# Two more FFN columns by seven products, single down tiles beside four columns, and a third last tile begun ahead

## The reference

```
up = rmsnorm(x) @ w_up                  # 1024 -> 2 x 2816: gate half and up half
c = conv_w3(up)                         # causal, depthwise, three taps
x = x + (silu(c_gate) * c_up) @ w_down  # 2816 -> 1024
y = rmsnorm(x)
```

## Time and profile before

| what | value |
|---|---|
| median of three runs | 858.47 us (856.91 to 859.96) |
| profiled execution, its own time | 860.1 us |
| its span, first to last instruction | 858.3 us |
| busy: PE, PEld, DVE, ACT, POOL | 839.3, 789.6, 570.7, 403.1, 124.5 us |
| mean granted clock of TensorE | 0.996 |
| first product of the first pair | 538 us |
| a pair's weight load (x<-in_w_up, 512 KB), issue to landing | 4.6 us, 30 of them |
| load of x behind the last sum (x<-scratch_x), issue to landing | 9.1 us, 2 of them |

### The profile page before, as it was taken

How to read it: one execution, slowest core, us unless ns; L and a number is a source line. 1 busy time by engine, 2 the same in 40 slices (tenths; PEclk the granted TensorE clock), 3 DMA queues, 4 the chain that set the end, 5 groups by cost and what they waited for, 6 DMA issues and landing times.

```text
span 858.3 us, 17439 instructions
## 1 busy us (share of the span) xinstructions
PE 839.3 (98%) x6800; PEld 789.6 (92%) x6800; DVE 570.7 (66%) x1005; ACT 403.1 (47%) x719; POOL 124.5 (15%) x181
## 2 busy tenths in 40 slices
PE   7999999999999999999999999999999999999995
PEld 7988877789999999877699999999999999999995
DVE  6444237578584643455354799899798998998654
ACT  7302133366353631255243665655555656656352
POOL 2320000000000000000000122323222423332100
PEclk9999999999999999999999999999999999999998
DMA  9798699721233465479232343754456656655623
GB/s 312 253 361 299 206 345 324 266 76 50 74 83 118 147 246 196 139 271 368 107 114 76 90 188 99 180 157 103 112 116 130 149 119 123 138 129 105 181 88 104
DMA packets 55188, 144.63 MB, mean 169 GB/s; under 512 B 6499, under 2 KB 9063, under 8 KB 54466
## 3 DMA queue, kind: packets, MB, share of 16 engines
q1 hardware_dynamic: 48496, 128.86, 45.3%
q0 software_dynamic: 6320, 14.53, 10.0%
q10 hardware_dynamic: 290, 0.12, 0.1%
HBM read 125.35 MB, written 18.14 MB: 167 GB/s over the span
## 4 chain that ended last, share of the span: by engine, by line
PE 81%; DMA 1%; DVE 1%; ACT 1%; issue 0%; DVEq 0%; SPq 0%
PE proj L1210 44%; PE score L1292 4%; PE score L1293 4%; PE score L1294 4%; PE T L1292 3%; PE T L1293 3%; PE T L1294 3%; PE proj L1166 2%; PE proj L1227 2%; PE proj L1229 2%; PE proj L1228 2%; PE score L1461 2%; PE score L1427 1%; DMA c_pages<-in_cache_mem_v 1%; PE T L1303 1%; PE T L1446 1%
## 5 line engine op out<-in xcount | busy, mean ns | idle before, releaser
L1210 PE MATMUL proj<-a_hi,w_hi 128*128 128x272 f32 (+1 forms) x740 | 159.8, 290 | 6.3 <-DVE w_lo L1928 6.1
L1210 PE MATMUL proj<-a_lo,w_hi 128*128 128x272 f32 (+1 forms) x740 | 158.5, 289 | 0.0
L1210 PE MATMUL proj<-a_hi,w_lo 128*128 128x272 f32 (+1 forms) x740 | 158.1, 288 | 0.0
L1561 ACT ACTIVATE w_hi<-w_raw 128x1024 fp32r<-128x1024 f32 (+2 forms) x114 | 104.6, 918 | 111.8 <-PE proj L1210 87.6
L1905 DVE TENSOR_TENSOR w_lo<-w_raw,w_hi 128x1024 fp32r<-128x1024 f32 (+2 forms) x114 | 119.8, 1051 | 30.0 <-ACT w_hi L1561 29.7
L1210 PEld LDWEIGHTS proj<-a_hi,w_hi 128*128 128x128 f32 x740 | 118.6, 190 | 12.7 <-issue 6.5
L1210 PEld LDWEIGHTS proj<-a_lo,w_hi 128*128 128x128 f32 x740 | 119.0, 190 | 0.0
L1210 PEld LDWEIGHTS proj<-a_hi,w_lo 128*128 128x128 f32 x740 | 118.7, 190 | 0.0
L1142 POOL COPY f_state<-up_pad 128x18 f32<-128x18 f32 x44 | 51.9, 1180 | 136.4 <-DVE up_pad L2061 136.4
L1857 ACT ACTIVATE p_hi<-x 128x1024 fp32r<-128x1024 f32 x30 | 31.6, 1055 | 37.4 <-PE T L1294 34.2
L1227 PE MATMUL proj<-a_hi,w_hi 128*128 128x272 f32 x160 | 48.0, 300 | 0.0
(11 more groups left out here) (364 smaller groups left out, 2055.9 us busy)
## 6 DMA issues: line engine op xcount, KB each, us to landing
x<-in_w_up SPq DMA_DIRECT2D x30, 512.0 KB, 4.6
w_raw<-in_w_in SPq DMA_DIRECT2D x21, 512.0 KB, 3.8
early_pages<-in_cache_k SPq DMA_DIRECT2D x32, 256.0 KB, 6.0
pages<-in_cache_v SPq DMA_DIRECT2D x32, 256.0 KB, 5.3
c_pages<-in_cache_mem_k SPq DMA_DIRECT2D x16, 512.0 KB, 6.6
c_pages<-in_cache_mem_v SPq DMA_DIRECT2D x16, 512.0 KB, 6.1
w_raw<-in_w_down SPq DMA_DIRECT2D x32, 256.0 KB, 2.7
w_raw<-in_w_up SPq DMA_DIRECT2D x14, 512.0 KB, 3.6
```

Source lines behind the costliest of these rows:

```text
L1210: mm = pe.matmul(tile_banks(n)[:, half, 0:width], wt, act[:, at, half * HALF:half * HALF + width], start=(k == 0 and a == 0), stop=(k == w ...
L1561: act.activation(w_hi[:, n % W_HI_RING, 0:kt, :], w_raw[:, n % W_RING, 0:kt, :], ACT.Copy).then_inc(w_hi_ready, 1)
```

## The change

`PAIRED` becomes 5 to 21, so columns 8 and 21 are computed by seven products. Down tiles stand beside columns 4 to 21, and columns 7, 8, 20 and 21 get one each. For these four a new branch gives another order: products 1, 2, down tile, 6, 5, 7, 3, 4; and on DVE output 7, then split 0 of the next pair, then its sums, then act (i-1). In column 21, which prepares no pair, act (20) stands ahead of output 7. SP's loads of raw pair weights wait for the sums too, product 6 for t_lo. Three last down tiles are begun ahead, the third in the bank pair `score`, with its weights split in column 21; w_hi and w_lo of the fourth tile come behind the start of the second.

```diff
--- before.py
+++ after.py
@@ -39,7 +39,7 @@
 GROUPS, GB = 2, 4
 SELF_UNITS = SEQ // P * HEADS
 FFN_GROUPS = [range(0, 4), range(4, 8), range(8, 12), range(12, 16), range(16, 22)]
-PAIRED = [i for i in range(5, 21) if i != 8]
+PAIRED = list(range(5, 22))
 DIST = 384
 W_RING, W_HI_RING = 4, 3
 C_PAGE_RING = 8
@@ -89,11 +89,18 @@
 
 def beside_of(i):
 
-    hosts = [c for c in range(4, 21) if c != 8]
-    if i not in hosts:
-        return []
-    g, j = divmod(hosts.index(i), 4)
-    return [(f"down{g}", "add", n) for n in (2 * j, 2 * j + 1)]
+    dealt = 0
+    for c in range(4, 22):
+        count = 1 if c in (7, 8, 20, 21) else 2
+        if c == i:
+            return [(f"down{m // KT}", "add", m % KT) for m in range(dealt, dealt + count)]
+        dealt += count
+    return []
+
+
+def by_act(q):
+
+    return (1, 5, 6, 4) if len(beside_of(PAIRED[q])) == 2 else (1, 6, 5, 4)
 
 
 def make_ffn_order():
@@ -104,7 +111,7 @@
             beside = beside_of(i)
             if i in PAIRED:
                 q = PAIRED.index(i)
-                order += [("prod", q, r) for r in (1, 2)] + beside[:1] + [("prod", q, r) for r in (5, 6)]
+                order += [("prod", q, r) for r in (1, 2)] + beside[:1] + [("prod", q, r) for r in by_act(q)[1:3]]
                 order += beside[1:] + [("prod", q, r) for r in (7, 3, 4)]
             else:
                 order += [("up", "gate", i), ("up", "up", i)] + beside
@@ -160,7 +167,7 @@
 VALUES = range(TILE["mem", "value", 0], TILE["mem", "value", KT - 1] + 1)
 FFN_FIRST = TILE[FFN_ORDER[0]]
 PRODUCTS = [(q, r) for phase, q, r in FFN_ORDER if phase == "prod"]
-BY_ACT, BY_DVE = (1, 5, 6, 4), (2, 7, 3)
+BY_DVE = (2, 7, 3)
 
 
 def make_schedule():
@@ -365,6 +372,21 @@
             s += [("prod", q, 1), ("prod", q, 2)]
             if prev_paired:
                 s += pair_ends(i - 1, q)
+            if len(downs) == 1:
+                hi0, lo0 = split_next(downs[0])
+                s += [("pair_out", q, 1), ("pair_out", q, 2), ("tile", downs[0])] + hi0 + [("taps", i - 1, 0)] + lo0
+                s += [("taps", i - 1, 1), ("gate", i - 1), ("prod", q, 6), ("prod", q, 5), ("pair_out", q, 6), ("add", downs[0])]
+                s += [("pair_out", q, 5)] + [("act", i - 1)] * (not more) + [("pair_hi", q + 1, 0)] * more
+                if i == FT - 1:
+                    s.append(("x_back",))
+                s += [("prod", q, 7), ("pair_out", q, 7)] + [("pair_split", q + 1, 0), ("sums", q + 1), ("act", i - 1)] * more + [("prod", q, 3)]
+                s += [("pair_hi", q + 1, 1)] * more + [("pair_out", q, 3), ("up_in", i, 0), ("prod", q, 4)]
+                if more:
+                    s.append(("pair_load", q + 2, 0))
+                if i == FT - 1:
+                    s += [("w_hi", TILE[LAST_DOWN, "add", 2]), ("w_lo", TILE[LAST_DOWN, "add", 2])]
+                    s += [("taps", i, 0), ("pair_out", q, 4), ("up_in", i, 1), ("taps", i, 1), ("gate", i), ("act", i)]
+                continue
             (hi0, lo0), (hi1, lo1) = (split_next(f) for f in downs)
             s += [("pair_out", q, 1), ("pair_out", q, 2), ("tile", downs[0])] + hi0
             if prev_paired:
@@ -411,10 +433,10 @@
             s += [("tile", f)] + hi + lo + [("add", f)]
         s.append(("act", i))
 
-    s += [("half_tile", TILE[LAST_DOWN, "add", n]) for n in range(2)]
+    s += [("half_tile", TILE[LAST_DOWN, "add", n]) for n in range(3)]
     for n in range(KT - 1):
         f = TILE[LAST_DOWN, "add", n]
-        hi, lo = split_next(f)
+        hi, lo = split_next(f) if n else ([], [])
         s += [("tile", f)] + hi + lo + [("add", f)]
         if 0 < n < KT - 1:
             s += [("squares", n - 1, "x"), ("apply", "final", n - 1)]
@@ -700,11 +722,11 @@
         proj = [ctx.enter_context(nc.psum_tensor(f"proj{i}", [P, 2, 512], F32)) for i in range(2)]
         score = ctx.enter_context(nc.psum_tensor("score", [P, 2, 512], F32))
         bank = {"S0": score[:, 0, :], "S1": score[:, 1, :], "Y0": proj[1][:, 0, :], "SB": proj[1][:, 1, :]}
-        THIRD = TILE["in", "q", 2]
+        THIRD, THIRD_LAST = TILE["in", "q", 2], TILE[LAST_DOWN, "add", 2]
 
         def tile_banks(n):
 
-            return score if n == THIRD else proj[n % 2]
+            return score if n in (THIRD, THIRD_LAST) else proj[n % 2]
 
         unit_bank = [proj[0][:, 0, 0:HALF], proj[0][:, 1, 0:HALF], proj[1][:, 0, 0:HALF]]
         for name in ("T0", "T1"):
@@ -768,8 +790,8 @@
 
         def wait_pair_out(eng, q, r):
 
-            if r in BY_ACT:
-                eng.wait_ge(sem("pair_copied"), len(BY_ACT) * q + BY_ACT.index(r) + 1)
+            if r not in BY_DVE:
+                eng.wait_ge(sem("pair_copied"), 4 * q + by_act(q).index(r) + 1)
             else:
                 eng.wait_ge(part_out, 2 * len(BY_HALF) + len(BY_DVE) * q + BY_DVE.index(r) + 1)
 
@@ -995,6 +1017,7 @@
                     j = step[2]
                     if arg:
                         wait_pair_lo(sp, arg - 1, j)
+                        sp.wait_ge(sem("sums_made"), arg)
                     else:
                         wait_x_free(sp)
                     sp.dma_start(p_raw[:, j, :, :], t["w_up"][((D_FF, 0)[j] + PAIRED[arg] * P) // P, :, :, :]
@@ -1184,6 +1207,9 @@
                 elif n == CO_FIRST + 1:
                     wait_taken(pe, "Y0", latest["Y0"])
                     wait_taken(pe, "SB", latest["SB"])
+                elif n == THIRD_LAST:
+                    wait_pair_out(pe, len(PAIRED) - 1, 3)
+                    wait_pair_out(pe, len(PAIRED) - 1, 4)
                 elif n >= 2 and n != THIRD:
                     wait_tile_out(pe, n - 2)
                 width = HALF if w["phase"] != "mem" else N_MEM
@@ -1266,6 +1292,7 @@
                     else:
                         pe.wait_ge(sem("blend_lo"), 4)
                 if r == 6:
+                    wait_pair_lo(pe, q, 2)
                     wait_pair_out(pe, q, 1)
                 if r == 7:
                     wait_pair_lo(pe, q, 1)
@@ -1855,7 +1882,7 @@
                         wait_product(act, q - 1, (2, 3, 4)[part])
                     src, dst = (t_raw[:, :, :, :], t_hi[:, :, :, :]) if part == 2 else (p_raw[:, part, :, :], p_hi[:, part, :, :])
                     act.activation(dst, src, ACT.Copy).then_inc(sem("pair_hi"), 1)
-                elif kind == "pair_out" and step[2] in BY_ACT:
+                elif kind == "pair_out" and step[2] not in BY_DVE:
                     q, r = step[1:]
                     wait_product(act, q, r)
                     if q:
@@ -2033,7 +2060,7 @@
                     split_lo(arg)
                 elif kind == "add" and arg not in X_ADDS:
                     dve.wait_ge(sem(f"x_loaded{TILES[arg]['i'] // 4}"), 32)
-                    out, held = proj[arg % 2], halves(x[:, TILES[arg]["i"], :])
+                    out, held = tile_banks(arg), halves(x[:, TILES[arg]["i"], :])
                     dve.wait_ge(tile_done, arg + 1)
                     dve.tensor_tensor(held, out[:, :, 0:HALF], held, ALU.add).then_inc(tile_out[arg % 2], 1)
                 elif kind == "up_in":
```

## The result

| | before | after |
|---|---|---|
| median of 20 runs each | 857.64 us (856.53 to 859.96) | 859.75 us (858.57 to 862.22) |
| ratio | | 1.0022, 95% interval 1.0015 to 1.0029 |
| profiled execution, its span | 860.1, 858.3 us | 858.64, 856.9 us |
| first product of the first pair | 537.97 us | 534.73 us |
| from there to the last norm's last matmuls (PE's row `score<-norm_area,ones`, x2) | 310.79 us | 313.21 us |

A forecast was written before the change was run, and what follows sets the result against it. TensorE was taken to bound the kernel. Matmuls saved (-3.0 us), stalls around columns 8 and 9 (+2.2) and in column 21 (+2.0), and the tail (+1.0) gave +2.2 us: 858.47 becomes 860.7 us, range 857.6 to 862.7.

The forecast's parts named there:

- The bound: FFN stage: TensorE sets the pace, busy for 98% of the span; VectorE is next, at 14.91 of 16.55 us a column.
- The saving: Columns 8 and 21: 96 matmuls become 84 in each, taking 3.01 us off TensorE.
- Column 7: VectorE idles 2.1 us ahead of product 7's output and ends its work 3.26 us into column 8.
- t_lo in columns 8, 9 and 21: VectorE's split of the sums comes late, stalling TensorE 1.0 us at product 6 (columns 8, 21) and product 5 (column 9).
- The free lag of 2.2 us: At a column's start VectorE may be up to 2.2 us late without TensorE waiting for t_lo.
- Product 4: TensorE waits for the output of product 7: 0.2 us in column 9, 1.0 us in column 21.
- The tail: Last down tiles: tile 3 waits 1.4 us for tile 1's add, where before there were 0.4, so 1.0 us more.
- What the third tile covers: Behind column 21's product 4: three half tiles (11.3 us) cover the 7.9 us to the last a_lo; two fall 0.4 short.
- The sum: Whole kernel: -3.0 + 2.2 + 2.0 + 1.0 = +2.2 us, giving a median of 860.7 us.
- The hidden lag: Rival, columns 8, 9 and 21: VectorE is under 2.2 us late, only the tail's 1.0 us stands, 856.5 us; chance 0.18.
- ScalarE: Rival, three late columns: ScalarE is late as well, up to another 0.8 us each, 863.1 us; chance 0.13.
- The clock: Rival: the clock falls to 1.2 GHz for one whole column, 13.5 us lost, 874 us; chance 0.02.

The follow-up runs named there:

- e7: e6 with output 4 and up_in (21, 1) moved ahead of taps (21, 0); ratio 0.9963 against the kernel before.
- e8: The changed kernel with two of the four adds of the sums left out for columns 8 and 21; ratio 0.9996 against the kernel before.
- e5: e1 with, in column 8, two of the four adds ahead of output 7 and two behind the next split; ratio 0.9975 against the kernel before.
- e2: The changed kernel with two last down tiles begun ahead instead of three; ratio 1.0011 against the kernel before.
- e6: e5 with two last down tiles begun ahead instead of three; ratio 0.9983 against the kernel before.
- e1: The changed kernel with the next pair's sums ahead of output 7 again in columns 7, 8 and 20; ratio 0.9986 against the kernel before.

## Why the prediction was right, point by point

- *The bound.* PE sets the pace; from 6800 to 6776 matmuls, and e7 keeps 2.5 us of what they save.
- *The saving* was mis-sized: 2.86 us, forecast 3.01. The stretch in the earlier trace rows that was read as column 8 began 0.13 us ahead of it. These are the first matmuls of columns 8 and 9 in the kernel before:
```profile
587.63 0.41 PE L1210 MATMUL proj<-d_hi,w_hi 128*128 128x272 f32 x2
...
599.59 0.29 PE L1292 MATMUL score<-d_hi,p_hi 128*128 128x272 f32 x1
```
So column 8 takes 11.96 us, not 12.1, and column 21 11.95 (798.18 to 810.13): 0.1246 us a matmul in an unpaired column, against 0.1254 in a paired one. As pairs they take 84 x 0.1254 = 10.53 us, and each saves 1.43. By the pace in the Trainium skill (TensorE: Matmul & The Clock Gate, "Wait — 56ns, not 53.3ns?") the estimate was 2.8 us, nearer to the 2.86, but not for its reason: neither kind of column ran at 116 ns a matmul.
- *Column 7.* DVE idle 2.0 us (2.1 in the working); it hands over at 3.28 us (3.26).
- *t_lo in columns 8, 9 and 21.* 1.0 us each, as forecast: 0.90 of hole and 0.10 behind it. Here two errors of 0.1 cancel, which is luck. PE goes on 0.04 us behind t_lo's end (588.25 to 588.29 in column 8), not 0.15, so the hole is shorter than forecast; and the 0.10 behind it was not in the forecast. The free lag of 2.2 us is shown by both sides: 3.3 stalls, 1.95 (e8) and about 2.1 (e5) don't.
- *Product 4.* In column 21 1.06 us with the 0.10 behind the hole, forecast 1.0. In column 9 the trace has 0.16 us, forecast 0.2; it is too short for the list of waits.
- *The tail.* The fourth tile's hole is 1.38 us from start to start for 0.39 before, +1.0 as forecast. DVE's rows, add 0, w_lo, add 1, stand as in the earlier trace rows:
```profile
820.61 0.72 DVE L2065 TENSOR_TENSOR x<-proj,x 128x544 f32<-128x544 f32 x1 [4.22 <-PE proj L1236]
821.48 0.96 DVE L1932 TENSOR_TENSOR w_lo<-w_raw,w_hi 128x768 fp32r<-128x768 f32 x1
822.36 0.71 DVE L2065 TENSOR_TENSOR x<-proj,x 128x544 f32<-128x544 f32 x1
```
- *What the third tile covers* was mis-sized. I priced two halves as short by 0.4; e2 and e6 measured 0.8 and 1.1 from start to start. The forecast costed the chain on DVE as a sum of its steps and left out ScalarE's first tap ahead of taps (21, 0). With w_lo in the chain DVE still waits 0.21 us for it, without w_lo 1.08, which is why the expectations of e2 and e6 missed as well. So the third tile costs 1.0 and gives 0.8 to 1.1: next to nothing in either order, not a loss by itself.
- *The sum.* By the holes in the trace it is 4.1 + 0.2 + 1.0 - 2.9 = +2.4 us, and PE reaches the last matmuls 2.42 us later. The forecast was 2.2, mainly because it put the saving 0.15 us too high. Up to the end it is 1.84, because the trace after is 0.6 us shorter behind the last matmuls, for which the forecast had no term. The ratio says 1.9 (1.3 to 2.5), which holds both. The forecast's 2.2 is 0.2 under the one and 0.4 over the other, so its nearness to the ratio is partly chance; the waits, their places and their sizes are what it had right.
- *The rivals.* The hidden lag fell: its condition, under 2.2 us, was not met. ScalarE was not late; in the table it has over 5 us idle in column 8, and the waits name DVE. The clock stayed at 1.00.

## What to carry to other kernels

When work is taken from the bounding engine, sum the next engine's work over each shortened stretch, but then walk its queue as well: here the total fitted well enough to lose almost nothing (0.35 us in e7), and a 2 us hole ahead of one early-placed output made four stalls of 1 us, of which another order (e1) takes back 3.2 us. A step that waits for a late result belongs behind the work that is ready, unless somebody waits for it sooner than that work takes. And a chain between two engines is not the sum of one engine's steps: taking a step out that stood in a wait gains nothing, moving one into a wait does.

## What was not expected

- A wait costs PE about 0.10 us more than its hole: the second matmul behind it comes 0.23 us after the first in place of 0.125, in all four places. At the fourth last tile it is 0.20 us in place of 0.125, before and after alike.
- The time ahead of the first pair differs by 3.2 us between two profiled executions (537.97 and 534.73 us) though the change leaves the work there as it is; over the ten traces the first product starts anywhere from 534.73 to 537.97. Comparing spans of single profiles would have given the change the wrong sign.
- The end behind the last matmuls is 0.6 us longer in the trace of the kernel before than in the nine others, which agree within 0.1. The two smallest stores of the result take 4.3 us from issue to landing in it (median), 3.6 in the kernel after. The nine ratios of the table lie at -0.5 us against before on average, as the column to the end does, and the column to the last matmuls is at +0.1. That speaks for something that the kernel before does every time, but it has one profile, and no run shows the cause.
